# The router's product on centred, unscaled rows: fp32 operands, root and bias applied at the logits

## What is computed

```python
h = layer_norm(DEEPNORM_ALPHA * h + t, ln_g[i, 0], ln_b[i, 0])
# layer_norm: (x - mean) * rsqrt(var + 1e-5) * g + b
logits = xt @ w_router + b_router            # xt = h, 256 x 1024; w_router 1024 x 32
top_logit, top_e = lax.top_k(logits, 4)
gate = softmax(top_logit)
# every expert: swiglu of (rows @ w_gu[e] + b_gu[e]), @ w_down[e] + b_down[e], weighted by gate
h = layer_norm(DEEPNORM_ALPHA * h + f, ln_g[i, 1], ln_b[i, 1])
```

## Time and profile before

| | |
|---|---|
| median of 3 runs | 2106.8 us |
| lowest and highest run | 2104.11 and 2107.93 us |
| the profiled execution: time | 2106.25 us |
| its span in the trace | 2104.5 us |
| granted clock of PE, mean | 0.99 of full speed |
| busy, share of the span | PE 96%, PEld 66%, DVE 43%, ACT 33%, POOL 2% |
| DMA | 604.26 MB, 287 GB/s on average |

### The profile page before, as it was taken

How to read it: one execution, slowest core, us unless ns; L and a number is a source line. 1 busy time by engine, 2 the same in 40 slices (tenths; PEclk the granted TensorE clock), 3 DMA queues, 4 the chain that set the end, 5 groups by cost and what they waited for, 6 DMA issues and landing times.

```text
span 2104.5 us, 28170 instructions
## 1 busy us (share of the span) xinstructions
PE 2015.3 (96%) x12131; PEld 1391.5 (66%) x12131; DVE 899.4 (43%) x1070; ACT 694.5 (33%) x955; POOL 41.9 (2%) x30
## 2 busy tenths in 40 slices
PE   8999999999999998999999999999999999999997
PEld 7999778999999886899888544443343333334432
DVE  5766665666666677656644411111111111111102
ACT  4545575444554556443444111110010000101101
POOL 2500000000000000000000000000000000000000
PEclk9999999999999998999999999999999999999999
DMA  9654607555555542455377899999999999999996
GB/s 303 203 196 150 230 1 244 194 182 180 180 180 180 191 149 79 161 193 187 101 260 272 339 426 428 427 428 428 428 427 427 428 427 428 427 427 428 427 428 291
DMA packets 165400, 604.26 MB, mean 287 GB/s; under 512 B 9268, under 2 KB 102400, under 8 KB 140500
## 3 DMA queue, kind: packets, MB, share of 16 engines
q1 hardware_dynamic: 165300, 602.82, 73.6%
HBM read 601.70 MB, written 1.09 MB: 286 GB/s over the span
## 4 chain that ended last, share of the span: by engine, by line
PE 71%; DMA 22%; DVE 3%; ACT 3%; issue 1%; SPq 0%; DVEq 0%; ACTq 0%
PE ps L1733 15%; PE ps L1735 15%; PE ps L1734 15%; PE ps L2209 11%; PE ps L2229 5%; DMA sb_raw<-in_moe_w_gate_up 5%; DMA sb_w_free<-in_moe_w_gate_up 3%; DMA sb_late_raw<-in_moe_w_down 3%; DMA sb_nat_more<-in_moe_w_gate_up 3%; DMA sb_w_free<-in_moe_w_down 3%; DMA sb_raw<-in_moe_w_down 3%; PE ps L2179 2%; PE ps L2237 1%; PE ps L2190 1%; ACT sb_w_hi L656 1%; PE ps L1925 1%
## 5 line engine op out<-in xcount | busy, mean ns | idle before, releaser
L1063 DVE TENSOR_TENSOR sb_w_lo<-sb_raw,sb_w_hi 128x2048 fp32r<-128x2048 f32 x179 | 415.0, 2323 | 275.7 <-ACT sb_w_hi L656 275.3
L656 ACT ACTIVATE sb_w_hi<-sb_raw 128x2048 fp32r<-128x2048 f32 x179 | 341.1, 1911 | 189.7 <-PE ps L1735 180.2
L1733 PE MATMUL ps<-sb_xT_hi,sb_w_hi 128*128 128x256 f32 x1408 | 397.0, 282 | 6.4 <-DVE sb_xT_lo L1087 4.4
L1735 PE MATMUL ps<-sb_xT_hi,sb_w_lo 128*128 128x256 f32 x1408 | 395.7, 281 | 0.0
L1734 PE MATMUL ps<-sb_xT_lo,sb_w_hi 128*128 128x256 f32 x1408 | 395.5, 281 | 0.0
L1733 PEld LDWEIGHTS ps<-sb_xT_hi,sb_w_hi 128*128 128x128 f32 x1408 | 266.3, 189 | 9.3 <-issue 4.4
L1734 PEld LDWEIGHTS ps<-sb_xT_lo,sb_w_hi 128*128 128x128 f32 x1408 | 266.3, 189 | 1.5
L1735 PEld LDWEIGHTS ps<-sb_xT_hi,sb_w_lo 128*128 128x128 f32 x1408 | 266.3, 189 | 0.0
L989 ACT ACTIVATE sb_h_rows<-ps 128x512 f32<-128x512 f32 x32 | 19.2, 599 | 417.6 <-PE ps L2209 417.6
L1618 DVE COPY sb_h_rows<-ps 128x512 f32<-128x512 f32 x31 | 21.4, 692 | 312.5 <-PE ps L2209 312.5
L1733 PE MATMUL ps<-sb_w_hi,sb_xT_hi 128*128 128x512 f32 x384 | 154.0, 401 | 0.3 <-DVE sb_xT_lo L1083 0.2
(11 more groups left out here) (305 smaller groups left out, 2448.5 us busy)
## 6 DMA issues: line engine op xcount, KB each, us to landing
sb_raw<-in_moe_w_gate_up SPq DMA_DIRECT2D x49, 2048.0 KB, 34.3
sb_w_free<-in_moe_w_gate_up SPq DMA_DIRECT2D x46, 2048.0 KB, 34.6
sb_w_free<-in_moe_w_down SPq DMA_DIRECT2D x23, 2048.0 KB, 34.1
sb_raw<-in_moe_w_down SPq DMA_DIRECT2D x23, 2048.0 KB, 34.0
sb_raw<-in_ffn_w_gate SPq DMA_DIRECT2D x44, 1024.0 KB, 5.2
sb_raw<-in_ffn_w_up SPq DMA_DIRECT2D x44, 1024.0 KB, 5.2
sb_raw<-in_ffn_w_down SPq DMA_DIRECT2D x44, 1024.0 KB, 4.9
sb_late_raw<-in_moe_w_gate_up SPq DMA_DIRECT2D x17, 2048.0 KB, 33.6
```

The lines of the kernel that those rows point to most:

```text
L656: sc.activation(w_hi[:, c % CUT, :], raw[:, c % RAW, :], ACT.Copy).then_inc(hi_made, 1)
L1063: ve.tensor_tensor(w_lo[:, c % CUT, :], raw[:, c % RAW, :], w_hi[:, c % CUT, :].bitcast(F32), ALU.subtract).then_inc(lo_made, 1)
L1733: pe.matmul(o, l_hi, r_hi, start=start, stop=False)
L1735: return pe.matmul(o, l_lo, r_hi, start=False, stop=stop)
```

## The change

- `wr2` and the cutting of the router's weights are gone; the router's weights stay in fp32 (`wr`).
- `centre` runs in two halves of 512 columns and waits for the loaded gains. PE transposes the centred rows of a block, half by half (`turn_centred`), ACT copies them to `centred_T`, and eight fp32 products of 128x128 weights and 32 columns give the block's unscaled logits (`logits(b)`), with rows on the partitions; there is no fold any more.
- The layer norm's bias is loaded once more, as eight rows of `grow`, by a ninth small DMA at the start, and becomes eight columns of `gcol`. Eight further fp32 products, with a column of it spread over 128 as weights, give its share of the logits (`bias_logits`); DVE adds that to the router's bias.
- DVE brings in 1/root at the logits, with one operation for each block, in place of one addition.
- The rows are scaled in halves (`norm_rows(b, h)`): the first halves before the logits are read, the second halves in `first_step`, between the second and the third gathered copy. PE waits for them ahead of the gather that follows the first gate/up chunk.
- Of the residual products one stays behind the logits, one goes into `first_step` ahead of the first gate/up chunk, two go into step 0 ahead of its `scatter`.
- Fills: two at a time in three places, where sixteen and four stood. The Exp table is loaded behind ACT's copies; the Sigmoid table's load waits for the exponent by a semaphore.

```diff
@@ -182,6 +181,9 @@
...
         late.close()
+        router_turned = ExitStack()
+        centred_T = sb("centred_T", [P, TB, KT, P], stack=router_turned)
+        router_turned.close()
         turned_rows = ExitStack()
...
@@ -456,6 +457,8 @@
...
                              bass.AP(a[name].tensor, a[name].offset, [[HD, n], [0, 2], [1, HD]])).then_inc(rows_loaded, 16)
+
+            sp.dma_start(grow[70:78, :], a["ln_b_2"][0, 0].rearrange("(k p) -> k p", p=P)).then_inc(rows_loaded, 16)
...
@@ -872,6 +875,10 @@
...
                     sc.activation(stat[:, 4 + b:5 + b], stat[:, 2 + b:3 + b], ACT.Sqrt).then_inc(ln_std, 1)
+                    for h in range(2):
+                        sc.wait_ge(rows_turned, 2 * b + h + 1)
+                        sc.activation(centred_T[:, b, 4 * h:4 * h + 4, :].rearrange("p k t -> p (k t)"), ps[:, 2 * b + h, :],
+                                      ACT.Copy).then_inc(rows_copied, 1)
                 sc.wait_ge(ln_std, TB)
@@ -974,12 +981,7 @@
...
             project(g_moba_out, c_moba_out, range(2), None)
-            sc.wait_ge(moe_loaded, MOE_LOADS)
-            sc.activation(wr2[:, :, 0, :], wr[:], ACT.Copy).then_inc(wr_cut, 1)
             first_layer_norm()
-            turn(t_moe)
-            sc.wait_ge(logits_done, 1)
-            sc.activation(lgT[:], ps[0:2 * N_E, 0, 0:S], ACT.Copy).then_inc(logits_copied, 1)
             sc.wait_ge(shifted, TB)
...
@@ -1365,27 +1368,31 @@
...
                     ve.bn_aggr(mean_var[:, b, :], row_stats[:, b].rearrange("p a b -> p (a b)")).then_inc(first_ln_step, 1)
-                    ve.wait_ge(first_ln_step, 2 * b + 1)
+                    ve.wait_ge(first_ln_step, b + 1)
                     ve.tensor_scalar(stat[:, 2 + b:3 + b], mean_var[:, b, 1:2], LN_EPS, None, ALU.add).then_inc(ln_var, 1)
                 def centre(b):
-                    ve.scalar_tensor_tensor(out=x[:, b, :], in0=x[:, b, :], scalar=mean_var[:, b, 0:1],
-                                            in1=ln0_gain[:], op0=ALU.subtract, op1=ALU.mult).then_inc(first_ln_step, 1)
-
-                def scaled(b):
-                    ve.wait_ge(ln_std, b + 1)
-                    ve.reciprocal(stat[:, 6 + b:7 + b], stat[:, 4 + b:5 + b]).then_inc(rstd_made, 1)
-                    ve.wait_ge(rstd_made, TB * 8 + b + 1)
-                    ve.wait_ge(first_ln_step, 2 * b + 2)
-                    ve.scalar_tensor_tensor(out=x[:, b, :], in0=x[:, b, :], scalar=stat[:, 6 + b:7 + b],
-                                            in1=ln0_bias[:], op0=ALU.mult, op1=ALU.add).then_inc(ln_rows, 1)
+                    ve.wait_ge(moe_loaded, MOE_LOADS)
+                    for h in range(2):
+                        cols = slice(512 * h, 512 * (h + 1))
+                        ve.scalar_tensor_tensor(out=x[:, b, cols], in0=x[:, b, cols], scalar=mean_var[:, b, 0:1],
+                                                in1=ln0_gain[:, cols], op0=ALU.subtract, op1=ALU.mult).then_inc(centred, 1)
                 spread(b)
-                if b:
-                    scaled(0)
                 centre(b)
-                if b:
-                    scaled(1)
+
+            def first_roots(b):
+
+                ve.wait_ge(ln_std, b + 1)
+                ve.reciprocal(stat[:, 6 + b:7 + b], stat[:, 4 + b:5 + b]).then_inc(rstd_made, 1)
+
+            def norm_rows(b, h):
+
+                ve.wait_ge(rstd_made, TB * 8 + b + 1)
+                ve.wait_ge(rows_turned, 2 * b + h + 1)
+                cols = slice(512 * h, 512 * (h + 1))
+                ve.scalar_tensor_tensor(out=x[:, b, cols], in0=x[:, b, cols], scalar=stat[:, 6 + b:7 + b],
+                                        in1=ln0_bias[:, cols], op0=ALU.mult, op1=ALU.add).then_inc(rows_normed, 1)
...
@@ -1570,7 +1568,9 @@
...
-            ve.wait_ge(logits_done, 1)
+            for b in range(TB):
+                first_roots(b)
+                norm_rows(b, 0)
             bias_rows(0, 0)
@@ -1581,10 +1581,12 @@
...
-            route(ve.memset(needles[:, :, TOP_K:8], BIG))
-            ve.wait_ge(logits_folded, 1)
-            route(ve.tensor_tensor(lg[:], ps[:, 0, S:S + TB * N_E].rearrange("p (b e) -> p b e", b=TB),
-                                   lg_row[:].unsqueeze(1).to_broadcast([P, TB, N_E]), ALU.add))
+            ve.wait_ge(bias_logits, 1)
+            route(ve.memset(needles[:, :, TOP_K:8], BIG),
+                  ve.tensor_tensor(lg_row[:], lg_row[:], ps[:, 7, 0:N_E], ALU.add))
+            ve.wait_ge(logits_done, 1)
+            route(*[ve.scalar_tensor_tensor(out=lg[:, b, :], in0=ps[:, 0, b * N_E:(b + 1) * N_E], scalar=stat[:, 6 + b:7 + b],
+                                            in1=lg_row[:], op0=ALU.mult, op1=ALU.add) for b in range(TB)])
             route(*[ve.max(top8[:, b, :], lg[:, b, :]) for b in range(TB)])
@@ -1666,6 +1668,9 @@
...
                 for j in range(4):
+                    if j == 2 and isinstance(r, int):
+                        norm_rows(0, 1)
+                        norm_rows(1, 1)
                     gathered_rows(g + j, 2 + j % 2, 0, 2 * j, 2)
@@ -2036,8 +2041,8 @@
...
             pe.wait_ge(ident_loaded, 16)
-            pe.wait_ge(rows_loaded, 16 * 8)
-            pe.transpose(ps[:, 0, 0:70], grow[0:70, :], ident[0:70, 0:70]).then_inc(gcol_turned, 1)
+            pe.wait_ge(rows_loaded, 16 * 9)
+            pe.transpose(ps[:, 0, 0:78], grow[0:78, :], ident[0:78, 0:78]).then_inc(gcol_turned, 1)
             pe.wait_ge(qscale_made, 1)
@@ -2133,33 +2138,43 @@
...
-            keep_busy_from_biases(2 * NORM_FILL, 7)
-
             def residual(b, h):
                 pe.wait_ge(scale_made, 1)
+                pe.wait_ge(rows_normed, 2 * h + b + 1)
                 pe.matmul(ps[:, 4 + 2 * b + h, :], grow[:], x[:, b, h * 512:(h + 1) * 512], start=True, stop=True)
-            turn(x, [(ln_rows, 1)], (0,))
+            def turn_centred(b):
+
+                for h in range(2):
+                    pe.wait_ge(centred, 2 * b + h + 1)
+                    for k in range(4):
+                        kk = 4 * h + k
+                        ins = pe.transpose(ps[:, 2 * b + h, k * P:(k + 1) * P], x[:, b, kk * P:(kk + 1) * P], ident[:])
+                    ins.then_inc(rows_turned, 1)
+
+            def logits(b):
+
+                for k in range(KT):
+                    if k % 4 == 0:
+                        pe.wait_ge(rows_copied, 2 * b + k // 4 + 1)
+                    ins = pe.matmul(ps[:, 0, b * N_E:(b + 1) * N_E], centred_T[:, b, k, :], wr[:, k, :],
+                                    start=k == 0, stop=k == KT - 1)
+                return ins
+
+            keep_busy_from_biases(2, 6)
+            turn_centred(0)
+            pe.wait_ge(moe_loaded, MOE_LOADS)
+            for k in range(KT):
+                ins = pe.matmul(ps[:, 7, 0:N_E], gcol[:, 70 + k:71 + k].to_broadcast([P, P]), wr[:, k, :], start=k == 0,
+                                stop=k == KT - 1)
+            ins.then_inc(bias_logits, 1)
+            logits(0)
+            turn_centred(1)
+            keep_busy_from_biases(2, 6)
+            logits(1).then_inc(logits_done, 1)
             residual(0, 0)
-            residual(0, 1)
-            turn(x, [(ln_rows, 2)], (1,))
-            pe.wait_ge(wr_ready, 1)
-            pe.wait_ge(turn_lo, 4 * t_moe + 1)
-            for k in range(KT):
-                turned_tile(t_moe, k)
-                w = wr2[:, k, :, :].rearrange("p a e -> p (a e)")
-                pe.matmul(ps[0:2 * N_E, 0, 0:S], w, xT_hi[:, k, :], start=k == 0, stop=False)
-                ins = pe.matmul(ps[0:2 * N_E, 0, 0:S], w, xT_lo[:, k, :], start=False, stop=k == KT - 1)
-            ins.then_inc(logits_done, 1)
-            residual(1, 0)
-            pe.wait_ge(logits_copied, 1)
-            for b in range(TB):
-                o = S + b * N_E
-                ins = pe.matmul(ps[:, 0, o:o + N_E], lgT[:, b * P:(b + 1) * P], fold_logits, start=True, stop=True)
-            ins.then_inc(logits_folded, 1)
-            residual(1, 1)
-            keep_busy_from_biases(4, 2)
+            keep_busy_from_biases(2, 6)
@@ -2264,10 +2279,14 @@
...
                 gather(3, 0, 2, 2)
+                if isinstance(r, int):
+                    residual(1, 0)
                 for j in range(4):
...
                     if j < 2:
+                        if isinstance(r, int):
+                            pe.wait_ge(rows_normed, 4)
                         gather(2 + j, 0, 4 + 2 * j, 2)
...
@@ -2321,6 +2340,9 @@
...
                     add_down_bias()
+                if residuals_here:
+                    residual(0, 1)
+                    residual(1, 1)
                 pe.wait_ge(y_lo_made, e + 1)
...
```

28 lines of the change are left out of this document (10 added, 18 removed).

## The result

The changed kernel takes 2087.2 us (median of five runs, 2082.41 to 2093.2) against 2106.6 for the kernel before (2104.11 to 2107.93, five runs). The ratio is 0.9905, with a 95% interval of 0.9895 to 0.9916: 0.95% or 19.4 us less. The forecast was 2.2 us less, with a range down to 2102.0. It missed by 17.4 us.

A forecast was written before the change was run, and what follows sets the result against it. Expert-stream DMA bandwidth was taken to set the end, with only its start movable by the router stage ahead; -3.5 + 0.86 + 0.47 = -2.2 us gave 2104.6 us, forecast's own range 2102.7 to 2106.5, with (b), (c), (d) 2102.0 to 2108.0.

The forecast's parts named there:

- the same starting point: Router stage rebuilt from PE being free at 1163.41 us, as in the profile of the kernel before.
- Two fills and eight transposes: PE at the router's start: two fills to 1163.86 us, then block 0's eight transposes to 1164.79.
- Thin products: Router's fp32 products of 32 columns: records 0.115 us apart, 1.84 us per group of sixteen, three groups.
- Rival (b): Router's weight loads don't overlap: 48 records at 0.187 us add 3.5 us, 2108.1 us; chance 0.09.
- rival (c): Router's thin products issue-bound at 0.05 us or below: logits 2.6 us earlier than forecast, 2102.0 us; chance 0.08.
- The logits reach DVE: End of the router's products: logits at DVE at 1171.98 us instead of 1175.50, 3.52 us earlier.
- The residual moved ahead of the first gate/up product: First expert step, between gathers and first product: two records cost 0.86 us in full.
- Start: One added small DMA at the kernel's start costs 0.47 us, carried to the router; bounds 0 and 0.8.
- The two residuals in step 0: Behind step 0's products: 1.72 us delaying later slot releases, hidden by 3 to 4 us of queued loads.
- Second-half scalings: Two of 0.68 us on DVE between second and third gathered copy: free; uncovered 1.4 us.
- (d): Expert layer: the end doesn't hang on the restart, only the added start remains, 2107.3 us; chance 0.11.
- (a): PE's clock falls in the router near 1170 us: up to 8.2 us more, 2112.8 us; chance 0.08.

The follow-up runs named there:

- e1: The kernel before with gcol 80 columns wide instead of 72, the last 8 never used; 2087.83 us, ratio 0.9919.
- e9: The kernel before with one unused tile of 32 bytes ahead of xT_hi, moving xT, a and all behind them; 2089.31 us, ratio 0.9921.
- e17: The kernel before with gcol 112 columns wide, the router of before; 2108.17 us.
- e18: The changed kernel with gcol 112 columns wide, run beside e17 at equal places; 2106.08 us.
- e2: The changed kernel with gcol 88 columns wide instead of 80; 2110.49 us, ratio 1.0014 against the kernel before.
- e8: The kernel before with one unused tile of 32 bytes ahead of w_hi, moving weights, x and all later tiles; 2107.52 us, ratio 1.000.

## Why the prediction was wrong, and where it was right

**The step that failed** stands in the sum's frame and not in one of its terms: "I rebuild it from the same starting point, PE free at 1163.41". The rebuilding was held against the kernel before, and all that comes ahead of that point was taken as it was, plus 0.47. The wider `gcol` counts in the list of changes as eight more columns to load and transpose; that a declared width moves each later tile was no step of the working, and no rival had it. It is worth 19.4 us by medians in e1 (2107.27 to 2087.83) and 16.9 in e9. From the profile of before alone the size couldn't be had. It does show that the pace of one product isn't fixed (118.7 and 117.3 ns in one pass), but nothing in it says that 113.6 exists. That the layout of operands of 6,432 PE-bound records was changed could have been said, with its price as unknown.

**The terms of the sum**, each from the first fill:

- Two fills and eight transposes: 1143.63 - 1142.31 = 1.32 us; forecast 1.38.
- Thin products: forecast 0.115 us apart. Measured 1.71/16 = 0.107 in the bias's group and 1.78/16 = 0.111 in each block's. Rival (b), 0.187, and rival (c), at most 0.05, are out. The Trainium skill, "TensorE: Matmul & The Clock Gate", Back-to-back issue gap, has 25 ns for such short products by themselves and says that in a stream of weight loads and products both set the spacing. The trace agrees with the latter: with 128 fp32 weight columns the records came 107 to 111 ns apart, and the sixteen weight loads of a group (PEld, 1.86 to 1.87 us) take as long as its products.
- The logits reach DVE 8.21 us after the first fill (1150.52) and not 8.57; before 12.09. So 3.88 earlier, forecast 3.52. The two narrow operations that replace one took 0.41 where 0.29 was put. The maxima, behind them, start 8.66 us after the first fill and not 12.35: 3.69 against 3.46.
- The residual moved ahead of the first gate/up product: the chain of waits after has it in full, at the length forecast.

```profile
1153.79 1.88 PE ps L2194 x16
1155.67 0.86 PE ps L2145 x2
1156.53 3.58 PE ps L2224 x16
```

- Start: PE's first instruction starts at 7.52 us, behind the new load, and at 7.38 before: 0.14 and not 0.47, within the bounds of 0 to 0.8. The issue itself took 0.42; the landing behind it was quicker. (The issues of before took 0.24 to 0.73 and not 0.42 to 0.73.)
- The two residuals in step 0: the eleventh load is issued 49.39 us after the restart (1209.55) and not 47.49. That is the 1.72 and a little, and it is hidden as forecast: DMA stays at 1.01 and 426 GB/s. (49 us from 1184.24 end at 1233 and not at 1235; with the 369 GB/s of the first 20 us the ten loads end near 1237, so the cover was there.)
- Second-half scalings: 1.40 us on DVE from 1156.05, under the first gate/up product, and the gather behind it starts without a wait at 1160.05.

With the start the terms come to -3.69 + 0.71 + 0.14 = -2.8 us in the profile (0.71: what follows the maxima was 8.48 and is 9.19 us long), against the forecast's -2.2 and 2.1 between e17's and e18's medians. **The mechanism and the size of the part that was worked out are right**; it is a ninth of what the change did.

**The rivals.** (d) is out: the end moved with the restart, 920.3 and 920.4 us behind it. (a) got a chance of 0.08 and does happen: 5.7 us in e2's stage, under the 8.2 that was put as its most, and six of eleven of e2's times lie in the upper group. In the changed kernel's own placement the two traces show none. The argument against it, that PE has hardly a gap there, doesn't hold: e2's PE was busy all of the 5.00 us ahead of the fall.

**What would have shown it wrong**, as the prediction listed it, was the stage only. The base time of 1163.41 was not on that list, and it is the first number that a comparison of the two traces shows.

## What to carry to other kernels

Read declarations in a diff as layout: a tile that grows by 32 bytes moves every later one, and where one engine's pace sets the time, its price is unknown in size and sign until it has been measured. To measure what an edit itself is worth, give the kernel before the same layout, with an unused tile of the same size, and compare that pair. And compare two traces first at the point where the changed stage begins, not inside it.

## What the runs showed of the hardware

- PE's pace for fp32r products hangs on where the operands stand in SBUF against each other, in steps of 32 bytes: 113.6 to 119.9 ns for 256 columns, 226.7 to 233.4 for 512, with idle 0.0. What counts is the distance (e8 moved weights and rows together and changed nothing), and the pace of 113.6 is back 256 and 1024 bytes on, but not 64 or 128.
- At one distance the pace can have two levels, 113.6 and 117.8 ns in the changed kernel and 117.3 and 118.7 in the kernel before, which change within one execution, mostly at a visit to another kind of product.
- A product of 32 columns with 128 fp32 weight columns costs two records of 0.107 to 0.111 us.
- The granted clock fell to 0.50 at the end of 5.00 us without a gap on PE (two wide fills, then transposes and fp32 products of 32 columns) in e2; in the changed kernel it stayed at 1.00 behind the same 45 records.
